# Two of the four weight sums of each second-layer gate/up block: from VectorE to two transfers

## The reference

```python
def _swiglu(x, w_gate, w_up, w_down):
    return (jax.nn.silu(x @ w_gate) * (x @ w_up)) @ w_down

for l in range(DEPTH):                                   # DEPTH = 2
    ...
    x = x + (gate_a * branch_a + gate_b * branch_b) @ w_o[l]
    x = x + _swiglu(_rmsnorm(x, norm2_g[l]), w_ffn_gate[l], w_ffn_up[l], w_ffn_down[l])
```

## Time and profile before

| what | us |
|---|---|
| median of 3 runs (1528.88 to 1531.28) | 1529.1 |
| the profiled execution, its own time | 1528.97 |
| its span in the trace | 1526.4 |
| TensorE busy | 1488.7 |
| VectorE busy | 1103.7 |
| GpSimd busy | 459.6 |
| first part, from the first result sum of block 0 to that of block 7 | 72.07 |
| second part, blocks 8 to 15, likewise | 69.40 |
| third part, blocks 16 to 21, likewise | 48.33 |

### The profile page before, as it was taken

The page is one execution under the profiler, slowest core; times in us unless marked ns, Lnnn a source line. Parts: engine busy times, 40 slices in busy tenths (PEclk is TensorE's granted clock), DMA queues, the critical chain, the costliest instruction groups (busy, mean ns, idle before and its releaser), DMA issues.

```text
span 1526.4 us, 22996 instructions
## 1 busy us (share of the span) xinstructions
PE 1488.7 (98%) x8944; PEld 1220.7 (80%) x8944; DVE 1103.7 (72%) x1469; ACT 670.4 (44%) x1145; POOL 459.6 (30%) x254
## 2 busy tenths in 40 slices
PE   8999999999999999999999999999998999999998
PEld 3555897778788878888888888878886998998997
DVE  5999888778348996558332881586878995896794
ACT  5464158852452222332332422688336552453361
POOL 0000053453444454343444423444541120110010
PEclk9999999999999999999999999999999999999999
DMA  6568720132233244453538642103322323234223
GB/s 248 164 206 296 285 79 1 51 116 83 97 113 111 71 164 155 142 163 89 177 103 291 210 142 90 42 1 84 101 91 71 111 90 132 83 97 139 71 92 116
DMA packets 73498, 189.50 MB, mean 124 GB/s; under 512 B 23600, under 2 KB 32176, under 8 KB 69296
## 3 DMA queue, kind: packets, MB, share of 16 engines
q1 hardware_dynamic: 41952, 145.18, 28.5%
q10 hardware_dynamic: 31440, 42.87, 8.7%
HBM read 155.52 MB, written 32.51 MB: 123 GB/s over the span
## 4 chain that ended last, share of the span: by engine, by line
PE 61%; DVE 21%; DVEq 6%; ACT 5%; issue 4%; POOLq 1%; DMA 1%; POOL 1%; ACTq 0%; SPq 0%
PE ps L2118 18%; PE ps L2120 18%; PE ps L2119 18%; DVE wl L1989 2%; PE ps L2267 2%; DVE wsum L1980 1%; DVE work L1372 1%; DVEq L1973 1%; PE ps L2244 1%; DVEq L1552 1%; DVEq L1981 1%; ACT prob L1147 1%; DVEq L1499 1%; ACT wh L729 1%; DVE wsum L1982 1%
## 5 line engine op out<-in xcount | busy, mean ns | idle before, releaser
L631 POOL TENSOR_TENSOR wl<-stage,wh 128x1024 fp32r<-128x1024 f32 x138 | 354.7, 2576 | 647.7 <-ACT wh L729 458.4
L729 ACT ACTIVATE wh<-stage 128x1024 fp32r<-128x1024 f32 (+2 forms) x178 | 181.0, 1023 | 219.5 <-PE ps L2120 100.3
L2118 PE MATMUL ps<-XH,wh 128*128 128x256 f32 x616 | 175.3, 285 | 7.8 <-DVE X L2010 5.0
L2120 PE MATMUL ps<-XH,wl 128*128 128x256 f32 x616 | 173.7, 282 | 0.0
L2119 PE MATMUL ps<-XLr,wh 128*128 128x256 f32 x528 | 148.7, 282 | 0.0
L2118 PE MATMUL ps<-xg2h,wh 128*128 128x512 f32 x352 | 140.2, 398 | 0.0
L2120 PE MATMUL ps<-xg2h,wl 128*128 128x512 f32 x352 | 139.2, 395 | 0.0
L2119 PE MATMUL ps<-xg2l,wh 128*128 128x512 f32 x352 | 139.2, 395 | 0.0
L2118 PEld LDWEIGHTS ps<-XH,wh 128*128 128x128 f32 x616 | 116.8, 190 | 10.6 <-DVE X L2010 5.4
L2120 PEld LDWEIGHTS ps<-XH,wl 128*128 128x128 f32 x616 | 116.8, 190 | 0.0
L2173 PE MATMUL ps<-X,slabs 128*128 128x512 f32 x224 | 101.8, 610 | 5.2 <-DMA X<-in_xT 5.2
(11 more groups left out here) (343 smaller groups left out, 3750.3 us busy)
## 6 DMA issues: line engine op xcount, KB each, us to landing
stage<-in_stream SPq DMA_DIRECT2D x178, 512.0 KB, 3.4
stage_more<-in_stream SPq DMA_DIRECT2D x34, 512.0 KB, 4.1
CPTR<-ctd_scr ACTq DMA_DIRECT2D x6, 1664.0 KB, 8.6
slabs<-in_stream SPq DMA_DIRECT2D x17, 512.0 KB, 4.9
InT<-in_scr ACTq DMA_DIRECT2D x6, 1024.0 KB, 6.7
ctd_scr<-CPp SPq DMA_DIRECT2D x4, 1152.0 KB, 7.9
ctd_scr<-CPp ACTq DMA_DIRECT2D x4, 1152.0 KB, 6.6
in_scr<-BPI SPq DMA_DIRECT2D x4, 1024.0 KB, 5.1
```

The costliest lines, as they stand in the source:

```text
L631: pool.tensor_tensor(wl[:, s, :], stage[:, (n - RAW) % STAGES, :], wh[:, s, :].bitcast(F32), ALU.subtract).then_inc(wl_ready, 1)
L729: return act.activation(o, i, ACT.Copy, **kw)
L2118: pe.matmul(o, wt[0], x[0], start=start, stop=False, skip_group_check=onto)
L2120: return pe.matmul(o, wt[1], x[0], start=False, stop=stop, skip_group_check=onto)
```

## The change

Two of the four sums, those in `wsum[1]` and `wsum[2]`, now come from transfers. A plain load issued by SyncE (`sums_base`) puts a quarter into each of the two places; an adding transfer issued by GpSimd (`sums_added`) adds one more quarter, the same to both. VectorE keeps one addition in `sums_first` and one in `sums_last`. The quarters are laid out in another order in the slabs, so that slot 0 comes from the second slab and slot 3 from the first, and the table of products follows. Two semaphores that counted copies of ScalarE become one.

```diff
-PRODUCTS = {"P2": (0, 0, X2), "P1": (0, 1, X1), "P5": (1, 0, X5), "P6": (1, 1, X6), "P3": (2, 0, X3),
-            "P7": (2, 1, X7), "P4": (3, 0, X4)}
+PRODUCTS = {"P2": (0, 0, X2), "P1": (0, 1, X1), "P5": (1, 1, X5), "P6": (1, 0, X6), "P3": (2, 1, X3),
+            "P7": (2, 0, X7), "P4": (3, 0, X4)}
...
             def freed_by_pair(q, i):
                 sp.wait_ge(s34_ready, q + 1)
-                if i:
+                if not i:
                     sp.wait_ge(op_lo[3], q + 1)
 
+            def sums_base(q):
+                z = LAST + pair_slab(q)
+                if q:
+                    sp.wait_ge(op_lo[2], q)
+                sp.dma_start(wsum[:, 1:3, :], stream[z:z + 2, :, QT:2 * QT].rearrange("i p c -> p i c"))\
+                    .then_inc(s13_loaded, 16)
+
+            sums_base(0)
             for z in range(2):
                 sp.wait_ge(wl_ready, LAST + z - STAGES + 1 - RAW)
                 fast_slab(z)
...
             for h in range(len(PARTS)):
                 for q in range(first_of(h), last_of(h) + 1):
+                    if q + 1 < FB:
+                        sums_base(q + 1)
                     for i in range(2):
...
+            def sums_added(q):
+                z = LAST + pair_slab(q)
+                pool.wait_ge(s13_loaded, 16 * (q + 1))
+                pool.dma_start(wsum[:, 1:3, :], stream[z, :, None, 0:QT].broadcast_to([P, 2, QT]),
+                               accum_op=ALU.add).then_inc(s13_ready, 16)
+
+            sums_added(0)
             for q in range(FB):
                 s = fast_slot(3)
                 pool.wait_ge(op_hi[3], q + 1)
-                pool.tensor_tensor(wl[:, s, 0:QT], fast_stage(pair_slab(q) + 1)[:, QT:2 * QT],
+                pool.tensor_tensor(wl[:, s, 0:QT], fast_stage(pair_slab(q))[:, QT:2 * QT],
                                    wh[:, s, 0:QT].bitcast(F32), ALU.subtract).then_inc(op_lo[3], 1)
+                if q + 1 < FB:
+                    sums_added(q + 1)
...
             def sums_first(q):
-                a, b = fast_stage(pair_slab(q)), fast_stage(pair_slab(q) + 1)
-                fast_loaded(pair_slab(q))
+                a = fast_stage(pair_slab(q) + 1)
                 fast_loaded(pair_slab(q) + 1)
+                dve.wait_ge(s13_ready, 16 * (q + 1))
                 dve.drain()
-                tt(wsum[:, 0, :], b[:, 0:QT], b[:, QT:2 * QT], ADD)
+                tt(wsum[:, 0, :], wsum[:, 1, :], a[:, QT:2 * QT], ADD).then_inc(s12_ready, 1)
+
+            def sums_last(q):
+                a = fast_stage(pair_slab(q) + 1)
                 dve.drain()
-                tt(wsum[:, 1, :], wsum[:, 0, :], a[:, QT:2 * QT], ADD).then_inc(s12_ready, 1)
-
-            def sums_last(q):
-                a, b = fast_stage(pair_slab(q)), fast_stage(pair_slab(q) + 1)
-                tt(wsum[:, 3, :], a[:, QT:2 * QT], b[:, 0:QT], ADD)
-                dve.drain()
-                tt(wsum[:, 2, :], wsum[:, 1, :], a[:, 0:QT], ADD).then_inc(s34_ready, 1)
+                tt(wsum[:, 3, :], wsum[:, 0, :], a[:, 0:QT], ADD).then_inc(s34_ready, 1)
...
-        blocks = (one[:, 1::2], one[:, 0::2], other[:, 0::2], other[:, 1::2])
+        blocks = (other[:, 0::2], other[:, 1::2], one[:, 1::2], one[:, 0::2])
```

More of the change, by code:

```diff
@@ L457, in build @@
         s34_ready = sem("s34_ready")
+        s13_loaded = sem("s13_loaded")
+        s13_ready = sem("s13_ready")
         op_hi = [sem(f"op_hi{i}") for i in range(4)]
@@ L460, in build @@
         prod_done = sem("prod_done")
-        p_copied = sem("p_copied")
-        five_copied = sem("five_copied")
+        half_copied = sem("half_copied")
         two_copied = sem("two_copied")
@@ L1246, in high @@
                 if i == 0:
-                    fast_loaded(pair_slab(q))
-                    copy(o, fast_stage(pair_slab(q))).then_inc(op_hi[0], 1)
+                    fast_loaded(pair_slab(q) + 1)
+                    copy(o, fast_stage(pair_slab(q) + 1)).then_inc(op_hi[0], 1)
                 elif i == 1:
@@ L1255, in high @@
                 else:
-                    fast_loaded(pair_slab(q) + 1)
-                    copy(o[:, 0:QT], fast_stage(pair_slab(q) + 1)[:, QT:2 * QT]).then_inc(op_hi[3], 1)
+                    fast_loaded(pair_slab(q))
+                    copy(o[:, 0:QT], fast_stage(pair_slab(q))[:, QT:2 * QT]).then_inc(op_hi[3], 1)
             def down_high(h, m):
@@ L1300, in first_copied @@
                     act.wait_ge(c11_done, q - 1)
-                copy(part_sums[:, q % 2, 0, :], ps[:, 4 + q % 2, 0:HTOK]).then_inc(p_copied, 1)
+                copy(part_sums[:, q % 2, 0, :], ps[:, 4 + q % 2, 0:HTOK]).then_inc(half_copied, 1)
             def five(q):
@@ L1306, in five @@
                     act.wait_ge(c22_done, q - 1)
-                copy(part_sums[:, q % 2, 1, :], ps[:, 6 + q % 2, 0:HTOK]).then_inc(five_copied, 1)
+                copy(part_sums[:, q % 2, 1, :], ps[:, 6 + q % 2, 0:HTOK]).then_inc(half_copied, 1)
             def two(q):
@@ L1969, in sums_first @@
             def sums_first(q):
-                a, b = fast_stage(pair_slab(q)), fast_stage(pair_slab(q) + 1)
-                fast_loaded(pair_slab(q))
+                a = fast_stage(pair_slab(q) + 1)
                 fast_loaded(pair_slab(q) + 1)
+                dve.wait_ge(s13_ready, 16 * (q + 1))
                 dve.drain()
-                tt(wsum[:, 0, :], b[:, 0:QT], b[:, QT:2 * QT], ADD)
+                tt(wsum[:, 0, :], wsum[:, 1, :], a[:, QT:2 * QT], ADD).then_inc(s12_ready, 1)
+            def sums_last(q):
+                a = fast_stage(pair_slab(q) + 1)
                 dve.drain()
-                tt(wsum[:, 1, :], wsum[:, 0, :], a[:, QT:2 * QT], ADD).then_inc(s12_ready, 1)
-            def sums_last(q):
-                a, b = fast_stage(pair_slab(q)), fast_stage(pair_slab(q) + 1)
-                tt(wsum[:, 3, :], a[:, QT:2 * QT], b[:, 0:QT], ADD)
-                dve.drain()
-                tt(wsum[:, 2, :], wsum[:, 1, :], a[:, 0:QT], ADD).then_inc(s34_ready, 1)
+                tt(wsum[:, 3, :], wsum[:, 0, :], a[:, 0:QT], ADD).then_inc(s34_ready, 1)
             def low(i, q):
                 s = fast_slot(i)
-                source = (fast_stage(pair_slab(q)), wsum[:, 0:2, :].rearrange("p i c -> p (i c)"),
+                source = (fast_stage(pair_slab(q) + 1), wsum[:, 0:2, :].rearrange("p i c -> p (i c)"),
                           wsum[:, 2:4, :].rearrange("p i c -> p (i c)"))[i]
@@ L2036, in first_sum @@
             def first_sum(q):
-                dve.wait_ge(p_copied, q + 1)
+                dve.wait_ge(half_copied, 2 * q + 1)
                 dve.wait_ge(prod_done, DONE[q, "P2"])
@@ L2045, in other_sums @@
                 dve.wait_ge(prod_done, DONE[q, "P7"])
-                dve.wait_ge(five_copied, q + 1)
+                dve.wait_ge(half_copied, 2 * q + 2)
                 tt(tile_of(q)[:, 1, HTOK:SEQ], part_sums[:, q % 2, 1, :], ps[:, 4 + q % 2, 0:HTOK], ADD).then_inc(c22_done, 1)
@@ L2618, in _ @@
                         corner(q - 1)
-                    pe.wait_ge(p_copied, q + 1)
+                    pe.wait_ge(half_copied, 2 * q + 1)
                     steps(q, "P6", range(4)).then_inc(prod_done, 1)
-                    pe.wait_ge(five_copied, q + 1)
+                    pe.wait_ge(half_copied, 2 * q + 2)
                     pe.wait_ge(op_lo[2], q + 1)
```

## The result

The changed kernel takes 1734.66 us (median, 1731.40 to 1741.18) against 1528.99 for the kernel before in the same comparison: ratio 1.1346, 95% interval 1.1324 to 1.1368. That is 205.7 us more. The forecast was 1716 us, range 1640 to 1780: direction, place and mechanism came out as worked out, and the sum was 19 us short. The profiled execution took 1732.03 us, its span 1730.2.

The account below looks back on a forecast made before the run. TensorE was taken to bound the kernel (1488.7 of 1526.4 us busy). Span 1526.4 + 186.2 (19 steps of 9.8) - 1.5 + 2.8 = 1713.9, plus 2.6 to the profiled execution: forecast 1716 us, range 1640 to 1780.

Parts of the forecast that it names:

- place and mechanism: On VectorE between `low(2, q)` and the next first sum: two whole transfers in series, uncovered, at 19 places.
- the sum: 19 steps between blocks at 9.8 us more, 186.2; less 1.5 at block 0, plus 2.8 for its reciprocal: span 1713.9.
- the second loop: Block cycle over TensorE and GpSimd: 12.3 us plus the adding transfer's 7.5, 19.8.
- the first: Block cycle over VectorE, plain load and adding transfer: 12.1 us plus 7.5, 19.6.
- The adding transfer: GpSimd's transfer into `wsum`, beside two slab loads: taken as 7.5 us, near three loads sharing at 7.3.
- the dear rival: Adding transfer between blocks at 10.5 us: cycle 22.8, time 1774; from 9.1 us on, 1747; chance 0.25.
- the reciprocal: Block 0's 3.34 us on VectorE, partly covered before, now inside the loop: about 2.8 us more.
- The start: Block 0: two VectorE sums leave the path, so TensorE starts this stage 1.5 us earlier.
- Cheap: Adding transfer between blocks at 3.1 us: time 1633; up to 5.5 us, below about 1679; chance 0.22.
- The clock staying up: TensorE's clock stays up in the pauses between blocks: cycle 19.6, time 1712, inside the forecast; no chance of its own.
- Hidden: Transfers land before VectorE reaches the next first sum; TensorE's 2.5 us of waits and 1.5 go: 1525; chance 0.02.

Follow-up runs that it names:

- the filler: Changed kernel with 64 matmuls that nobody reads added behind P7 of each block but a part's last: 1725.05 us.

## Why the prediction was right, and which terms were off

**The place and the mechanism** held at each sign named: 19 waits of VectorE ahead of the first sum, released by a DMA, 13 us each (a little over the 9 to 12 of the forecast); result sums 20.3 to 21.0 us apart (about 20), but for the first step of the stage and the last of each part; the lower clock in all three parts (0.73 to 0.76); the down stages at 46.2 us as before; line 1999 never at 1.8 us.

**The loop.** That the second loop is the longer was shown by leaving out the plain load, and that the first is right behind it by the filler. The second was put at 12.3 us plus the adding transfer, and took 12.6 in the block shown and 12.3 on average. Inside it the clock cost a little more (20 matmuls at 0.095 us more, not 16 at 0.09) and the hand-overs a little less.

**The adding transfer** was put at 7.5 us by three loads sharing (1.9 + 3 x 1.8) and landed after 8.2. This is the term most at fault, and that it came so near was partly luck: two errors took each other back. The sharing of three loads was priced too dear, for a plain transfer from GpSimd, beside the same two slab loads, landed after 5.8 us, where that working gives 7.3. And the addition was left out, which costs 2.4 in this company. Alone the adding transfer takes 5.3 us, not the 3.7 of a plain load, and the company costs it 2.9, not 3.6. The forecast had put all of it on the company and left the addition to the dear rival. The Trainium skill (DMA: Bandwidth & Descriptors, Anatomy of one DMA — SWDGE (gpsimd) path) gives an estimate of 3.2 us by its formula. The runs have 5.3 for the adding transfer alone, and 5.8 for a plain one from GpSimd beside two slab loads; none has the plain one alone, which is what the formula is for.

**The sum.** On TensorE the three parts grew by 77.0, 73.4 and 52.6 us (first matmul of a part to the first down product: 85.51, 78.52 and 58.22 before, 162.55, 151.91 and 110.79 after), 203.0 in all. In the second and third part that is 10.5 a step, where the forecast had 9.8, and the 0.7 is the adding transfer's 8.2 instead of 7.5. The first part has 3.5 us more than seven such steps; the reciprocal stands in it, which was put at 2.8. The span came out 16.3 us longer than forecast (1730.2 against 1713.9): 13.3 in the steps, 0.7 in the first part, 1.2 at the start, 1.1 behind the last block. The other 2 us of the 19 lie between the profiled execution and the median, which were 2.6 us apart.

**The start.** 1.5 us were forecast and the pause fell by 1.35 (4.01 instead of 5.35 between two starts). But the stage's first matmul came only 0.26 us earlier (1172.09 instead of 1172.35), as the products ahead of it ended 1.1 us later. In the traces of the other kernels with this start it came between 1170.1 and 1174.7, so one trace can't tell what the stage ahead lost to the early transfers, if anything.

**What the prediction didn't price** is the wait for `op_lo[3]`, now ahead of both slab loads. The forecast counted both slab loads as company of the adding transfer, but no term spoke of the slabs coming later. Here it was worth 9 us by one experiment, hidden behind the longer wait. Once that wait is gone it decides the sign: 1536.0 with it, 1524.8 without.

**The rivals.** Cheap and dear were wrong in size. The clock staying up was put at 1712; kept up by the added matmuls in 13 of the 19 steps it gave 1725, with the landing at 8.4 us and GpSimd waiting for the plain load besides. Hidden, put at 1525, was wrong for this kernel and right as a number: with a second copy, the sums later in the row and the slab loads exchanged the time is 1524.8. That is the rule in the Trainium skill (same page, Rules for kernel authors) to issue early and wait late; the trace agrees, since the same transfers, landing after 7.4 us, cost nothing there.

## What to carry to other kernels

Before work is moved from an engine to a transfer, look at what frees the destination and what reads it next. If one buffer serves both, the whole latency lies between two neighbours in a row, and the price of each step is the work from a landing to the next issue, plus the landing, minus the old cycle, whatever the engine saved. A second copy first, then the order of the other loads on the same queue, which may have inherited a wait. Moving the waiting instruction along its row did little here: 22 of the 206 us.

## What the runs showed of the hardware

- A transfer that adds 512 KB of float32 into on-chip memory lands after 5.3 us alone and 8.2 beside two loads of 512 KB. It has 272 packets where the plain one has 144, takes 3.0 us of all sixteen DMA engines instead of 1.6, and holds GpSimd for 1.20 us instead of 0.72. The plain one from GpSimd, beside the same two loads, lands after 5.8.
- Half of it, 256 KB, lands after 6.6 us in the same company and holds GpSimd for 0.87.
- One load beside it costs it nearly as much as two (median 7.9 and 8.2 us), but the landings spread more: 5.7 to 8.6 us from issue to the sum behind it, instead of 7.7 to 8.5.
- After a pause of 8.6 us TensorE did 20 matmuls 0.21 us apart, at the lower of its two levels (1.2 GHz), and only then 0.12 apart. That costs 1.9 us each time, but matmuls in the pause, which took the slow start out of 13 of 19 steps, brought back only 0.5 a step, as the other loop stood right behind.
- GpSimd's rest of 128x512 took 1.28 us with no VectorE instruction beside it and 1.86 where 0.7 us of VectorE's line 2071 or 2074 fell into it. Before the change, VectorE's line 1980 took 1.78 us beside such a rest, and its successor 0.69 by itself.
